# Deferring a norm's root behind the first products, and scaling the results by a row of roots

## The reference

```
h = rmsnorm(x, mix_pre_norm)                  # x * rsqrt(mean(x*x) + eps) * gain, over the 1024 channels
u = h @ w_in                                  # 1024 x 3072
u_a, u_b, hq, hk, hv, hg = split(u, 512 each)
y_conv = silu(layernorm(conv31(u_a * sigmoid(u_b)) + b))   # causal, 31 taps, one filter for each channel
q, k = rotary(hq), rotary(hk) ; v = hv        # 4 heads of 128
o = retention(q, k, v)                        # chunks of 128, decay by head
y_ret = silu(hg) * o * rsqrt(mean(o*o) + eps)
x = x + rmsnorm(concat(y_conv, y_ret) @ w_out, mix_post_norm)
```

## Time and profile before

| | us |
|---|---|
| median of 3 runs | 904.84 (904.33 to 904.93) |
| profiled execution, its own time | 903.12 |
| its span | 901.2 |
| busy: PE / DVE / ACT / POOL | 888.2 / 624.2 / 502.9 / 347.5 |

### The profile page before, as it was taken

How to read it: one execution, slowest core, us unless ns; L and a number is a source line. 1 busy time by engine, 2 the same in 40 slices (tenths; PEclk the granted TensorE clock), 3 DMA queues, 4 the chain that set the end, 5 groups by cost and what they waited for, 6 DMA issues and landing times.

```text
span 901.2 us, 15285 instructions
## 1 busy us (share of the span) xinstructions
PE 888.2 (99%) x6308; PEld 780.8 (87%) x6308; DVE 624.2 (69%) x812; ACT 502.9 (56%) x730; POOL 347.5 (39%) x133
## 2 busy tenths in 40 slices
PE   8999999999999999999999999999999999999997
PEld 7999877888888878999999988877788888888886
DVE  6999757888882267668799765753415689999623
ACT  7545646444454356655566565555545576666533
POOL 2981002666664400000000008546783166666542
PEclk9999999999999999999999999999999999999999
DMA  9762645555556545545545534444464465555551
GB/s 356 259 213 95 236 149 209 189 187 187 187 188 208 204 149 187 187 152 179 199 135 183 179 87 179 159 163 149 140 210 140 159 232 192 188 188 187 186 187 47
DMA packets 31014, 162.44 MB, mean 180 GB/s; under 512 B 9154, under 2 KB 10322, under 8 KB 12514
## 3 DMA queue, kind: packets, MB, share of 16 engines
q1 hardware_dynamic: 30738, 161.13, 51.8%
q10 hardware_dynamic: 144, 0.26, 0.1%
q0 software_dynamic: 64, 0.08, 0.0%
HBM read 160.20 MB, written 1.27 MB: 179 GB/s over the span
## 4 chain that ended last, share of the span: by engine, by line
PE 84%; DVE 9%; ACT 3%; DMA 2%; issue 1%; POOL 1%; SPq 0%; DVEq 0%; ACTq 0%
PE acc L1874 18%; PE ring L1739 15%; PE ring L2228 12%; PE ring L1773 9%; PE acc L1773 9%; PE ring L1777 5%; PE ring L1820 4%; PE acc L1777 4%; DVE acc L1281 4%; DMA raw<-wstream 2%; PE acc L2083 1%; PE acc L1887 1%; ACT w_hi L728 1%; DVE rope_b L1315 1%; DVE w_lo L1164 1%
## 5 line engine op out<-in xcount | busy, mean ns | idle before, releaser
L728 ACT CAST w_hi<-raw 128x1024 fp32r<-128x1024 f32 x284 | 297.1, 1052 | 315.4 <-PE ring L1739 78.0
L674 POOL TENSOR_TENSOR w_lo<-raw,w_hi 128x1024 fp32r<-128x1024 f32 x118 | 331.8, 2816 | 313.1 <-ACT w_hi L728 312.9
L1164 DVE TENSOR_TENSOR w_lo<-raw,w_hi 128x1024 fp32r<-128x1024 f32 x166 | 214.3, 1300 | 112.2 <-ACT w_hi L728 102.8
L1739 PE MATMUL ring<-h,w_hi 128*128 128x256 f32 x960 | 174.3, 284 | 1.0 <-issue 1.0
L1739 PEld LDWEIGHTS ring<-h,w_hi 128*128 128x128 f32 x960 | 149.8, 192 | 1.0 <-issue 0.7
L1739 PE MATMUL ring<-h,w_lo 128*128 128x256 f32 x480 | 136.1, 283 | 0.0
L1739 PEld LDWEIGHTS ring<-h,w_lo 128*128 128x128 f32 x480 | 92.2, 192 | 1.1 <-issue 1.1
L699 POOL TENSOR_SCALAR_AFFINE_SELECT toep_t<-toep_t 64x2304 f32<-64x2304 f32 x2 | 5.9, 2938 | 224.1 <-DMA toep_t<-toep 224.0
L1874 PE MATMUL acc<-w_hi,ff 128*128 128x512 f32 x340 | 91.2, 390 | 0.0
L1773 PE MATMUL ring<-h,w_hi 128*128 128x512 f32 x352 | 88.2, 393 | 0.0
L1773 PE MATMUL acc<-h,w_hi 128*128 128x512 f32 x336 | 84.6, 394 | 0.0
(11 more groups left out here) (292 smaller groups left out, 1372.2 us busy)
## 6 DMA issues: line engine op xcount, KB each, us to landing
raw<-wstream SPq DMA_DIRECT2D x142, 1024.0 KB, 4.9
toep_t<-toep SPq DMA_DIRECT2D x16, 96.0 KB, 3.1
x<-x_tok SPq DMA_DIRECT2D x2, 512.0 KB, 4.5
mem<-mem_tok SPq DMA_DIRECT2D x1, 1024.0 KB, 11.2
w_ple<-wproj SPq DMA_DIRECT2D x1, 1024.0 KB, 7.2
decay<-decay_tab SPq DMA_DIRECT2D x1, 768.0 KB, 6.4
out_t<-y SPq DMA_DIRECT2D x3, 256.0 KB, 2.1
u<-uconv SPq DMA_DIRECT2D x4, 142.0 KB, 5.8
```

Of the source, the lines that this page charges most:

```text
L674: nc.gpsimd.tensor_tensor(w_lo[:, u % UNITS], unit_of_raw(u), as_f32(w_hi[:, u % UNITS]), ALU.subtract).then_inc(lo_ready["pool"], 1)
L728: nc.scalar.copy(w_hi[:, u % UNITS], unit_of_raw(u)).then_inc(hi_ready, 1)
L1164: V.tensor_tensor(w_lo[:, u % UNITS], unit_of_raw(u), as_f32(w_hi[:, u % UNITS]), ALU.subtract).then_inc(lo_ready["dve"], 1)
L1739: last = mm(dst, w[a], src[:, b, kt], start=n == 0 and i == 0, stop=n == kts - 1 and i == 2)
```

## The change

x is also loaded by channel (`x_ch`, 128 partitions x 8 tiles x 256 tokens), as the first transfer. ACT, DVE and GpSimd multiply it with the gain of the channel (`pre_col`) and write `h` at once, unnormed; the eight low parts are DVE's. The gain row's product, the turns of x and the first norming are gone. `unnormed_pair` runs conv 0 with the low weights last. x by token is loaded later; ACT squares it, and DVE takes the reciprocal. Between the two tiles of conv 1, PE forms a row of the roots (two small products), DVE copies it to `r_row`. The root is then applied to the results: the conv banks and the g banks are scaled on DVE in PSUM (`row_scaled`), q and k by scaling the rotary table, v on ACT with the root as scale (`v_out`). mem's norming moves to ACT, without gain; its gain is applied in four pieces for each turned tile (`turned_hi`, `turned_lo`). The taps are spread anew, units 0 and 5 go from GpSimd to DVE, both mem splits go ahead of k's rotary, and the first tile of memk 1 goes ahead of the spread of the retention roots. PE runs 20 small products before conv 0. `first_lo` writes the low part of x times gain, 128x256 an instruction; `g_out` waits for the scaled bank and takes Silu.

```diff
-TAPS_FROM, TAPS_TO = 5, FIRST_BLOCK[INDEX[("g", 1)]] // UB
+TAPS_FROM, TAPS_TO = 6, FIRST_BLOCK[INDEX[("g", 1)]] // UB
-    if u == 0 or _within(u, _POOL_ONLY) or TAPS_FROM <= u < TAPS_TO:
+    if _within(u, _POOL_ONLY) or TAPS_FROM <= u < TAPS_TO:
...
+            sp.dma_start(y[:], x_ch).then_inc(load_xt, 16)
+            sp.dma_start(pre_col[:], pre).then_inc(load_pre, 16)
+            sp.dma_start(raw[:, 0, 0:UB], wstream[0][:, 0:UB]).then_inc(first_unit_ready, 16)
+            sp.dma_start(raw[:, 0, UB:], wstream[0][:, UB:]).then_inc(slot_ready[0], 16)
+            for n in range(1, NSLOTS):
...
+                if n == 1:
+                    sp.dma_start(x[:], x_tok).then_inc(load_x, 16)
+                    sp.dma_start(con[:, 0:P], consts[:, 0:P]).then_inc(load_ident, 16)
...
...
+            for k in range(XT_DVE, KT):
+                nc.gpsimd.tensor_scalar(h[:, 0, k], y[:, k], pre_col[:, k:k + 1], None, ALU.mult).then_inc(xt_hi_pool, 1)
...
+                if stage == "mem":
+                    for i in range(4):
+                        kt = 4 * (k % 2) + i
+                        ins = A(turned_h(stage, k, 0)[:, i], turned_bank(stage, k)[:, i], ACT.Identity,
+                                scale=pre_col[:, KT + kt:KT + kt + 1])
...
+            for k in range(XT_ACT):
+                A(h[:, 0, k], y[:, k], ACT.Identity, scale=pre_col[:, k:k + 1]).then_inc(xt_hi_act, 1)
+            act.wait_ge(first_unit_ready, 16)
+            nc.scalar.copy(w_hi[:, 0, 0:4], raw[:, 0, 0:4]).then_inc(first_cast, 1)
+            nc.scalar.copy(w_hi[:, 0, 4:8], raw[:, 0, 4:8]).then_inc(hi_ready, 1)
...
+            for tt in range(2):
+                n = NORM["mem", tt]
+                act.wait_ge(mem_inverse, tt + 1)
+                for half in range(2):
+                    c = slice(512 * half, 512 * half + 512)
+                    A(y_tok[:, tt, c], mem[:, tt, c], ACT.Identity, scale=sums[:, 2, n:n + 1]).then_inc(t_full, 1)
...
-            copy_fill("g", 0, g_ret[:, 0:2], ACT.Silu)
+            g_out(0)
             turned_hi("mem", 2)
...
+            for k in range(KT):
+                first_lo(k)
...
+            V.tensor_copy(r_row[:], st[:, 0:S]).then_inc(row_ready, 1)
+            def row_scaled(name, j, signal):
+                dve.wait_ge(pe_step, fill_step(fi(name, j)))
+                V.tensor_tensor(bank(name, j), bank(name, j), over(r_row[:], 2), ALU.mult).then_inc(signal, 1)
...
             for j in range(4):
                 gates[0] += 1
-                feed_behind("conv", j)
+                if j == 0:
+                    feed(TAPS_FROM - 1)
+                row_scaled("conv", j, conv_scaled)
+                if j == 1:
+                    feed(TAPS_FROM)
+                taps((0, 2, 3, 3)[j])
                 wait_gate(gates[0])
...
-                taps((8, 16, 14, 0)[j])
+                taps((0, 6, 8, 0)[j])
...
+            after(link(V.tensor_tensor(rope[:], rope[:], over(r_row[:], 2), ALU.mult)))
             rope_of(0, q_raw)
             turned_lo("mem", 0)
-            rope_of(1, k_raw)
             turned_lo("mem", 1)
...
+            rope_of(1, k_raw)
             feed_behind("v", 1)
...
+            row_scaled("g", 0, g_scaled)
             feed_behind("g", 0)
             turned_lo("mem", 2)
...
+            for _ in range(12):
+                mm(sc[2][:, 0:P], rstd[:, 0:P], rstd[:, 0:P], start=True, stop=True)
+            pe.wait_ge(load_xt, 16)
+            for _ in range(8):
+                mm(sc[2][:, 0:P], rstd[:, 0:P], rstd[:, 0:P], start=True, stop=True)
+            unnormed_pair("conv")
+            fill = open_fill("conv", 1)
+            tile_out(fill[:, 0], h)
...
+            pe.wait_ge(pre_inverse, 2)
+            for tt in range(2):
+                n = NORM["mix_pre", tt]
+                last = mm(st[:, tt * P:tt * P + P], sums[:, 2, n:n + 1].to_broadcast([P, P]), mat("ident"),
+                          start=True, stop=True)
+            last.then_inc(row_spread, 1)
+            tile_out(fill[:, 1], h)
```

More of the change, by code:

```diff
@@ L341, in program @@
         mix_keys = sem("mix_keys")
-        load_x = [sem(f"load_x{i}") for i in range(2)]
+        load_x = sem("load_x")
         load_ident = sem("load_ident")
@@ L824, in _ @@
             prime(ACT.Sqrt)
+            act.wait_ge(load_pre, 16)
+            act.wait_ge(load_xt, 16)
+            for k in range(XT_ACT):
[3 more added lines that the diff above has]
+            nc.scalar.copy(w_hi[:, 0, 4:8], raw[:, 0, 4:8]).then_inc(hi_ready, 1)
+            fed[0] = 1
+            act.wait_ge(slot_ready[0], 16)
+            feed(ahead_target(0))
+            act.wait_ge(load_x, 16)
             for tt in range(2):
-                act.wait_ge(load_x[tt], 16)
                 mean_square("mix_pre", tt, x[:, tt], q_tok[:, tt])
                 deviation("mix_pre", tt)
[L829 to L833, removed]
+            feed(split_target(fi("conv", 0)))
+            act.wait_ge(pe_step, fill_step(fi("conv", 0)))
+            feed(behind_target(fi("conv", 0)))
+            prime(ACT.Sigmoid)
+            act.wait_ge(load_params, 32)
+            for j in range(4):
+                wait_fill("conv", j)
+                act.wait_ge(conv_scaled, j + 1)
+                wait_gate_slot(act, "conv", j)
+                A(gate_tmp[:, gate_slot("conv", j), 0], bank("conv", j)[:, 1], ACT.Sigmoid).then_inc(gate_done, 1)
             act.wait_ge(load_mem, 16)
@@ L872, in _ @@
             turned_hi("mem", 3)
-            copy_fill("g", 1, g_ret[:, 2:4], ACT.Silu)
+            g_out(1)
             prime(ACT.Sqrt)
@@ L1317, in rope_of @@
                 V.tensor_tensor(t[:], rope_a[:], rope_b[:], ALU.add).then_inc(rope_ready, 1)
+            logits = vec[:, VEC["lb"]:VEC["lb"] + 16]
+            V.tensor_tensor(lb[:, 0], logits, logits, ALU.subtract).then_inc(lb_exp, 1)
+            taps(24)
+            for tt in range(2):
+                n = NORM["mem", tt]
+                dve.wait_ge(dev_ready, n + 1)
+                V.reciprocal(sums[:, 2, n:n + 1], sums[:, 1, n:n + 1]).then_inc(mem_inverse, 1)
             taps(CW * (4 - len(PACKED)))
             dve.wait_ge(load_side, 48)
+            after(link(V.tensor_tensor(rope[:], rope[:], over(r_row[:], 2), ALU.mult)))
             rope_of(0, q_raw)
             turned_lo("mem", 0)
-            rope_of(1, k_raw)
             turned_lo("mem", 1)
@@ L1740, in tile_out, with unnormed_pair @@
                     step(last, at_block[0])
+            def unnormed_pair(name):
+                b = open_fill(name, 0)
+                first = at_block[0] // UB
+                at_block[0] += 2 * UB
+                for i in range(2):
+                    for part in range(2):
+                        for kt in range(KT):
+                            if i == 0 and part:
+                                pe.wait_ge(xt_lo, kt + 1)
+                            elif i == 0 and kt < XT_ACT:
+                                pe.wait_ge(xt_hi_act, kt + 1)
+                            elif i == 0 and kt < XT_DVE:
+                                pe.wait_ge(xt_hi_dve, kt - XT_ACT + 1)
+                            elif i == 0:
+                                pe.wait_ge(xt_hi_pool, kt - XT_DVE + 1)
+                            if i == 0 and part == 0 and kt == 0:
+                                pe.wait_ge(first_cast, 1)
+                            elif part == 0 and kt == (0 if i else 4):
+                                pe.wait_ge(hi_ready, first + i + 1)
+                            mm(b[:, i], w_hi[:, (first + i) % UNITS, kt], h[:, part, kt],
+                               start=i == 0 and part == 0 and kt == 0, stop=False)
+                for i in range(2):
+                    u = first + i
+                    pe.wait_ge(lo_ready[LO_ENGINE[u]], lo_count(u, LO_ENGINE[u]))
+                    for kt in range(KT):
+                        last = mm(b[:, i], w_lo[:, u % UNITS, kt], h[:, 0, kt], start=False, stop=i == 1 and kt == KT - 1)
+                    step(last, UB * (u + 1))
             def first_pair(name, j, stage):
@@ L1979, in _ @@
             last.then_inc(ret_spread, 1)
-            pair("memk", 1, mem_n)
+            tile_out(fill[:, 1], mem_n)
             def wout_ready(i, tt):
```

136 lines of the change are left out of this document (84 added, 52 removed).

## The result

The changed kernel takes 911.88 us (median of 4 runs, 909.36 to 913.5); the kernel before took 904.59 beside it (904.18 to 904.93). The ratio is 1.0077, 95% interval 1.0059 to 1.0095: a loss of 7.0 us by the ratio and of 7.3 by the medians. The forecast was 908.3, range 904.0 to 911.0: the sign was right, the size was half of what came. The profiled execution is the slowest of the four (913.5, span 911.5 against 901.2), so its rows show more than the median holds.

What follows compares the result with a forecast made beforehand. PE and the pair DVE/ACT were taken as both bounds up to 99.70 us; PE gains 3.0 us at the start, but the DVE/ACT chain puts the statistic 3.45 later: 904.84 + 3.45 = 908.3, range 904.0 to 911.0.

Steps and rivals of the forecast that it cites:

- the part after 110 us is rigid: After 110 us PE is busy 781.5 of 791 us; untouched by the change, this part moves as a block.
- The start: Up to "mem" turn 1: first product 8.8 instead of 12.1, PE 3.0 us earlier, turn 1 at 71.2 instead of 74.16.
- VectorE ahead of v: DVE before "mem" turn 1's split: taps end 64.1, only 0.9 us earlier; turn 0 split at 72.6, then 1.8 us idle.
- From v to the statistic: DVE/ACT chain behind v: decay products end at 94.95 instead of 92.2, statistic at 103.15 instead of 99.70, +3.45 us.
- TensorE's waits: PE waits 1.2 us before the scores, about 3 before decayed sums, 2 before memk, 1.5 at the statistic.
- That the shift is the same for the profiled execution and the median: The +3.45 us holds for the profiled run (903.12) and the median, so 904.84 + 3.45 = 908.3.
- B: At unit 5's split GpSimd gets ahead of DVE, which waits 2.4 us; v 1.7 us later, 910.0; chance 0.22.
- C: PE starts at the low clock, first 16 to 24 products doubled: up to 1.9 us on v, 910.2; chance 0.06.
- D: The new small pieces are cheap, near the low bounds: -0.4 to +1.8 us, 904.4 to 906.6; chance 0.20.
- A: The sum as forecast, with unit 5's spare time kept: 906.7 to 909.3; chance 0.40.
- E: From v to the statistic, DVE and ACT come forward with PE, so the 3 us survive: 901.9; chance 0.12.

Runs made afterwards that it cites:

- experiment 1: The changed kernel with the ring's PSUM banks turned by one, so every fill has its old bank: 906.08 us against 904.71, ratio 1.0019.
- experiment 2: The kernel before with only its banks turned as they lie in the changed kernel: 909.79 us, ratio 1.0058.
- experiment 5: On experiment 1's kernel, VectorE's scaling of the first g bank moved ahead of the reciprocal of the convolution's root: 905.39 us, ratio 1.0012.
- Experiment 7: The kernel before with experiment 6's order behind the decay products, where its statements exist: 903.96 us, ratio 0.9992.
- experiment 4: On experiment 1's kernel, the 20 small products at the start left out: 908.76 us, ratio 1.0043.
- experiment 8: On experiment 6's kernel, casts of units 26 and 27 between squares and table load, mem's second-turn high part ahead of v's copy: 900.35 us against 904.52.
- experiment 6: On experiment 5's kernel, mem's last high part ahead of the decay products' wait, table load behind the squares, casts behind the root: 903.23 us, ratio 0.9993.

## Why the prediction was right and wrong, step by step

- **The step that failed: "the part after 110 us is rigid".** It is rigid only while each fill follows the same bank's last reader. I counted four removed fills as work gone and never as four places gone from a list that deals out banks modulo 3. That is 5.2 of the 7.0 us by the ratios (experiments 1 and 2, from both sides): a wait of 4.5 us for a copy that the fill had not needed before, and the low clock behind it. The check was to be had before the run: 4 modulo 3 is not 0, and for each later fill, those with fixed banks above all, one asks who read its bank last.
- **The start: right.** Forecast and measured: first product 8.8 and 8.55, pair 1 14.75 and 14.29, "mem" turn 1 71.2 and 71.4; DVE's low halves of x took 3.38 us for 8, where 0.435 each gave 3.48.
- **VectorE ahead of v: two misses that cancel in part.** The taps ended at 65.56, not 64.1, and the row product on rope took 1.91 us at 65.48, where I had 0.68 and a hold of 2 us. VectorE came to the split of turn 1 at 73.4, not at 72.6, so it idled 1.07 us there, not 1.8.
- **From v to the statistic: right, term by term.** From v (71.40) the turned high part took 3.07 us (3.25 forecast), the four small pieces 1.12 (1.2), the mean 1.59 (1.6), k's rotary 4.88 (4.9), the rest to the end of the decay products 12.69 (12.8), and from there to the statistic 8.10 (8.2). Decay products' end 94.95 forecast, 92.77 + 1.94 = 94.71 measured; statistic 103.15 and 102.81; so +3.45 and +3.1.
- **TensorE's waits: their number, sum and place were off.** I had four, 7.7 us together (1.2, 3, 2, 1.5); there were three in that stretch, 4.8 together (0.5, 2.81, 1.54). The last was exact. The large one stood at a turn, not at the decayed sums, because that turn needs the first g pair's bank, which I had left out of the account. My four waits were also 0.7 more than the 7.0 that my own shift allowed (3.0 + 3.45 + the 0.52 of before). The missing 2.9 are in part the 1.5 us by which the lower clock stretched the half of g 1 behind that wait: in experiment 1 it ran 91.21 to 95.65, 4.44 us, before 90.58 to 93.53. I had priced no wait at a second price for the clock; in the front experiment 5 shows that this price was not what held the statistic.
- **That the shift is the same for the profiled execution and the median: wrong, and in the other direction.** The front alone (experiment 1) is +3.0 in the profiled pair and +1.4 by the medians (1.0019: 1.7). The profiled execution of before, 903.12, lay 1.7 under its median of 904.84. The shift was read from that execution and belonged on its time: 903.12 + 3.45 = 906.6, where experiment 1 has 906.18 in its profiled run and 906.08 as median. Added to the median it made the front's term twice too large, which by luck hid a part of the missing banks. Experiment 7's profiled run (903.3 for 901.2) shows two things that may vary in that kernel: x at 7.76 where the earlier trace rows has 7.20, with the merge's fill 0.6 later, and a wait of 1.2 us in the merge for a low part of GpSimd's. How often either comes was not measured.
- **Rivals.** B (GpSimd ahead at unit 5) did not occur: VectorE began 0.08 us before it, and had its split in 1.22 us; GpSimd took 8.14 us for three. That is closer than the account could tell, so its absence here is luck, and experiment 4, where GpSimd was 0.02 us ahead, shows its whole price.

```profile
22.28 1.22 DVE L1223 TENSOR_TENSOR w_lo<-raw,w_hi 128x1024 fp32r<-128x1024 f32 x1
22.36 8.14 POOL L688 TENSOR_TENSOR w_lo<-raw,w_hi 128x1024 fp32r<-128x1024 f32 x3 [13.46 <-ACT w_hi L748]
```

  C is what experiment 4 shows without the small products, 1.7 us at the first 32; with them it did not come. D fell: the four pieces cost 1.14 us on ScalarE and 1.12 on VectorE, near the 1.2 taken and far above their low bounds. A's mechanism held in the front (+3.1). E (all comes forward) was not the change's result, but experiment 8 shows that 97.9 at the statistic can be passed (97.16) once ScalarE's order is mended. My argument against E priced the queue as written and took it for a bound of the work.
- The range left 911.88 out by 0.9. It covered the front's unknowns, with B's and C's prices as they came out in experiment 4, and held no term for the part that I had declared fixed.

## What to carry to other kernels

When a change adds or removes an entry of a list from which buffers are dealt in turn, write out for every later entry which buffer it gets and who read that one last, before and after. Look first at entries with fixed buffers: where those meet the ones dealt in turn, a shift of the count changes who waits for whom. When a queue gains work, look first for what in it nobody waits for yet: here 4.4 us of casts, a table load and a turned part stood ahead of the four squares that held TensorE. And a wait of TensorE can cost twice, once for itself and once for the clock behind it, where the time hangs on TensorE (at 559 us); where it hangs on another queue (at 91 us), removing both gave 0.8 us. A shift that is read from one profiled execution is added to that execution's time, not to a median.

## What was not expected of the hardware

- After TensorE's wait of 4.50 us its granted clock read 0.50 for over 4 us and products ran at half pace, +2.9 us; in experiment 2, after 4.98 us, it read 0.50 over 2.5 us and 0.90 over the next 2, +1.3 us; after 2.81 us it read 0.66 over 5 us, and TensorE's stretch there was 1.5 us longer. So the price of such a gap differs between runs; with 18 small products in the wait it stayed at 1.00. The Trainium skill, TensorE: Matmul & The Clock Gate, Part 1: The HAM clock gate, has an idle array fall from 2.4 to 1.2 GHz; the rows agree.
- In experiment 4 the granted clock reads 1.00 at the start while 17 products take 3.64 us, twice the later time of each. There the pace of the products, not the clock column, tells the level.
- Where VectorE and GpSimd both take the split of a unit, the rows show one waiting for the whole of the other's instruction, and a lead of 0.02 us decides: in experiment 4 GpSimd began first and took 2.40 us, VectorE 3.46 (1.06 more than GpSimd's); in the changed kernel VectorE began 0.08 us ahead and took its usual 1.22 us.
- ScalarE's squares ran straight behind a Silu, with no table load between them; that let the load go behind the squares. The Trainium skill, ScalarE: Activation LUTs, section Table sets: the hidden batching unit, has cheap functions (it lists relu, copy, identity and abs) in every set; the trace of experiment 6 shows no load ahead of Square either, which that list does not name:

```profile
95.64 0.60 ACT L933 ACTIVATE g_ret<-ring 128x512 f32<-128x512 f32 x1 [0.50 <-DVE ring L1381]
96.14 0.38 ACT L936 ACTIVATE sq<-acc 128x256 f32<-128x256 f32 x1
```
